# A decoder step on one core: mixed tiles kept in SBUF, sums of squares inside the output product, half of a norm's remainders on GpSimd

## The reference

```
att   = rmsnorm(diff_attention(...), g_head) * (1 - lam_init)
glu   = gelu(s5_scan(...)) @ w_glu
mixed = sigmoid(gate_a) * (att @ w_attn_up) + sigmoid(gate_s) * (glu[:2048] * sigmoid(glu[2048:]))
x     = x + mixed @ w_out
h     = rmsnorm(x, g_ffn)
x     = x + peer_ffn(h)      # queries h @ w_query, product keys, 128 x 128 single-neuron experts
x     = x + (p @ w_ple) * sigmoid(rmsnorm(x, g_ple) @ w_ple_gate)
```

## Time and profile before

| what | us |
| --- | --- |
| median of 3 runs | 4635.27 (4634.18 to 4642.76) |
| the profiled execution | 4642.33 |
| its span | 4640.6 |
| TensorE busy (matmuls) | 4358.9 (94%) |
| DVE busy | 2641.2 (57%) |
| GpSimd busy | 2535.1 (55%) |
| ACT busy | 1537.7 (33%) |

### The profile page before, as it was taken

How to read it: one execution, slowest core, us unless ns; L and a number is a source line. 1 busy time by engine, 2 the same in 40 slices (tenths; PEclk the granted TensorE clock), 3 DMA queues, 4 the chain that set the end, 5 groups by cost and what they waited for, 6 DMA issues and landing times. The chain is left out here.

```text
span 4640.6 us, 80519 instructions
## 1 busy us (share of the span) xinstructions
PE 4358.9 (94%) x29764; PEld 4156.5 (90%) x29764; DVE 2641.2 (57%) x4339; ACT 1537.7 (33%) x2344; POOL 2535.1 (55%) x1826
## 2 busy tenths in 40 slices
PE   7899976999998898999999999999899999999999
PEld 5788875888787897999999999999899999999899
DVE  4477764554434302679566666655576767767621
ACT  3122213443443323223333333333333333333232
POOL 5687751322222342445566666657566666666543
PEclk9999987999999998999999999999899999999999
DMA  4233322334984532333589999979888888878533
GB/s 113 71 94 93 94 62 89 104 100 125 375 316 148 192 111 75 99 92 129 199 314 340 328 344 323 346 256 332 306 323 328 336 331 320 340 281 335 210 97 95
DMA packets 365052, 993.54 MB, mean 214 GB/s; under 512 B 43922, under 2 KB 121490, under 8 KB 305970
## 3 DMA queue, kind: packets, MB, share of 16 engines
q1 hardware_dynamic: 268370, 554.21, 36.1%
q0 software_dynamic: 46560, 337.14, 18.7%
q10 hardware_dynamic: 49920, 99.47, 5.6%
HBM read 904.93 MB, written 85.72 MB: 213 GB/s over the span
## 5 line engine op out<-in xcount | busy, mean ns | idle before, releaser
L2774 PE MATMUL val_y_ps<-val_wt,val_v 128*128 128x384 f32 x6144 | 1074.2, 335 | 30.4 <-DVE val_wt L2848 23.7
L2774 PEld LDWEIGHTS val_y_ps<-val_wt,val_v 128*128 128x128 f32 x6144 | 1068.0, 188 | 36.1 <-issue 31.4
L248 PE MATMUL rt_acc<-xn_act,rt_w_hi 128*128 128x384 f32 x4096 | 1062.8, 340 | 31.0 <-POOL rt_w_rest L238 30.7
L238 POOL TENSOR_TENSOR rt_w_rest<-rt_w_raw,rt_w_hi 128x512 fp32r<-128x512 f32 x576 | 736.9, 1304 | 509.5 <-ACT rt_w_hi L233 507.2
L248 PEld LDWEIGHTS rt_acc<-xn_act,rt_w_hi 128*128 128x128 f32 x4096 | 739.1, 188 | 46.3 <-POOL rt_w_rest L238 42.6
L2736 POOL TENSOR_TENSOR val_v<-val_v_raw,val_v 128x2048 fp32r<-128x2048 f32 x128 | 591.0, 4617 | 327.1 <-ACT val_v L2807 327.0
L248 PE MATMUL rt_acc<-xn_act,rt_w_rest 128*128 128x384 f32 x2048 | 691.8, 338 | 0.0
L2651 DVE CUSTOM_DVE_ANT_0 rt_space<-rt_space,rt_mid 128x2048 f32<-128x2048 f32 x160 | 360.9, 2280 | 216.1 <-DMA rt_space<-in_peer_u,out_row_id 208.5
L2869 DVE TENSOR_TENSOR out_xT<-out_xT,val_y_ps 128x384 f32<-128x384 f32 x512 | 282.3, 551 | 339.6 <-PE val_y_ps L2774 339.4
L233 ACT ACTIVATE rt_w_hi<-rt_w_raw 128x512 fp32r<-128x512 f32 x576 | 334.6, 627 | 283.3 <-PE rt_acc L248 196.7
L248 PEld LDWEIGHTS rt_acc<-xn_act,rt_w_rest 128*128 128x128 f32 x2048 | 383.7, 187 | 0.0
(11 more groups left out here) (428 smaller groups left out, 7308.8 us busy)
## 6 DMA issues: line engine op xcount, KB each, us to landing
rt_w_raw<-in_peer_uT SPq DMA_DIRECT2D x512, 256.0 KB, 5.2
val_v_raw<-in_peer_vp SPq DMA_DIRECT2D x128, 1024.0 KB, 5.0
scan_w_raw<-in_w_in SPq DMA_DIRECT2D x128, 256.0 KB, 3.2
att_w_raw<-in_w_in SPq DMA_DIRECT2D x96, 256.0 KB, 3.4
hid_scratch<-rt_hid ACTq DMA_DIRECT2D x128, 192.0 KB, 6.2
gate_scratch<-rt_space ACTq DMA_DIRECT2D x12, 2048.0 KB, 10.3
val_hid<-hid_scratch SPq DMA_DIRECT2D x32, 768.0 KB, 8.3
val_gate<-gate_scratch SPq DMA_DIRECT2D x32, 768.0 KB, 11.5
```

The costliest lines, as they stand in the source:

```text
L238: e.tensor_tensor(self.rest[:, s, 0:nk, :], self.raw[:, r, 0:nk, :], self.hi[:, s, 0:nk, :].bitcast(F32), ALU.subtract).then_inc(self.rest ...
L248: mm = e.matmul(acc[:, h, 0:width], w[:, s, k, :], act[:, kt0 + k, a, col + h * width:col + (h + 1) * width], start=first and k == 0 and w ...
L2774: mm = e.matmul(y_ps[:, t % 2, 0:DW], v[:, c % 2, a, j, t * P:(t + 1) * P], wt[:, g % 2, j, b, :], start=j == 0 and a == 0 and b == 0, sto ...
```

## The change

Four edits:

1. `xT` is allocated at the outset; `early` and `qk_sample` become views of it, since its 34 KB are just theirs. `stage_mix` writes the mixed tile straight into `xT[:, c]`. The ring `mix`, the 16 stores, their waits and `mix_dram` go. `stage_out` makes high part and remainder from `xT`, and fetches the residual's input over a pair of tiles once their remainders are made, after the loads of the odd column of the pair.
2. In `stage_out` ACT interleaves the splits of the first four weight units with the copies (after tiles 0, 4, 8 and 12 instead of 3, 7, 11 and 15). All loops are unrolled.
3. The squares and the sums over them move from the norm into `stage_out`: ACT squares tile c-2 after the first weight split of column c, and TensorE sums tile c-1 after the third unit of column c; the last two squares and the last sum stand at the end. The sums' accumulator `end` is allocated outside both stages.
4. In `Norm`, the ring of scaled tiles grows from 2 to 4; DVE scales one tile ahead; the remainders of odd tiles are made by GpSimd, after its fourth weight remainder; the query product waits for even and odd ones.

```diff
@@ -291,82 +291,69 @@
...
-    def squares(self, e, landed=None):
...
     def split(self, e):
-        e.wait_ge(self.sq_used, KT)
-        e.activation(halves(self.sq[:, 0, :]), self.total[:, :, 0:HALF], ACT.Copy, scale=1.0 / 32
+        e.activation(halves(self.part[:]), self.total[:, :, 0:HALF], ACT.Copy, scale=1.0 / 32
                      ).then_inc(self.part_ready, 1)
...
+        for t in range(KT):
+            e.wait_ge(self.scaled_ready, t + 1)
+            e.activation(self.out[:, t, 0, :], self.scaled[:, t % 4, :], ACT.Copy).then_inc(self.hi_ready, 1)
...
-        for k in range(KT):
-            e.wait_ge(self.sq_ready, k + 1)
-            square_sum(e, self.total, self.sq, self.c("ones"), k).then_inc(self.sq_used, 1)
...
     def wait_tiles(self, e, n):
-        e.wait_ge(self.scaled_free, n + 2)
+        e.wait_ge(self.rest_even, n // 2)
+        e.wait_ge(self.rest_odd, n // 2)
+    def rest(self, e, t, done):
+        e.wait_ge(self.hi_ready, t + 1)
+        e.tensor_tensor(self.out[:, t, 1, :], self.scaled[:, t % 4, :], self.out[:, t, 0, :].bitcast(F32),
+                        ALU.subtract).then_inc(done, 1)
+    def odd_rests(self, e):
+        for t in range(1, KT, 2):
+            self.rest(e, t, self.rest_odd)
     def vector(self, e):
         e.wait_ge(self.dev_ready, 1)
         e.reciprocal(self.rstd[:], self.deviation[:]).then_inc(self.rstd_ready, 1)
         e.wait_ge(self.rstd_ready, 1)
         e.wait_ge(self.gain_in, 16)
...
+        def scale(t):
+            if t >= 4:
+                e.wait_ge(self.rest_odd if t % 2 else self.rest_even, t // 2 - 1)
+            e.scalar_tensor_tensor(out=self.scaled[:, t % 4, :], in0=self.x[:, t, :], scalar=self.gain[:, t:t + 1],
+                                   in1=self.rstd[:], op0=ALU.mult, op1=ALU.mult).then_inc(self.scaled_ready, 1)
+        scale(0)
+        for t in range(0, KT, 2):
+            scale(t + 1)
+            if t + 2 < KT:
+                scale(t + 2)
+            self.rest(e, t, self.rest_even)
...
-                if part == ATT and c:
-                    store(c - 1)
-            store(KT - 1)
-            for a in range(2):
-                e.wait_ge(mix_stored[a], 16 * (KT // 2))
@@ -2074,12 +2051,10 @@
...
-                if c >= 2:
-                    e.wait_ge(mix_stored[c % 2], 16 * (c // 2))
...
-                e.tensor_tensor(mix[:, c % 2, :], a_part[:], x, ALU.add).then_inc(mix_ready, 1)
+                e.tensor_tensor(k.xT[:, c, :], a_part[:], x, ALU.add).then_inc(mix_ready, 1)
...
@@ -2098,82 +2073,86 @@
...
         @block.sync
         def _(e):
+            for c in range(KT):
+                for u in range(U):
+                    w.load(e, 0, 0, c * U + u, columns(k.w_out, c, UNIT * u))
+                if c % 2:
+                    e.wait_ge(rest_ready, c + 1)
+                    e.dma_start(k.xT[:, c - 1:c + 1, :], k.x_dram[:, c - 1:c + 1, :]).then_inc(x_in[c // 2], 16)
+        @block.gpsimd
+        def _(e):
+            w.credit_rest(e)
+            for u in range(KT * U):
+                w.split_rest(e, 0, 0, u)
+        @block.scalar
+        def _(e):
+            def square(t):
+                e.wait_ge(added, t + 3)
+                if t >= 4:
+                    e.wait_ge(sq_used, t - 3)
+                e.activation(sq[:, t % 4, :], k.xT[:, t, :], ACT.Square).then_inc(sq_ready, 1)
             for t in range(KT):
...
+                e.activation(k.act[:, t, 0, :], k.xT[:, t, :], ACT.Copy).then_inc(hi_ready, 1)
+                if t % UNIT == 0:
+                    w.split_hi(e, 0, 0, t // UNIT)
+            for u in range(RING, KT * U):
+                w.split_hi(e, 0, 0, u)
+                if u >= 2 * U and u % U == 0:
+                    square(u // U - 2)
+            for t in range(KT - 2, KT):
+                square(t)
         @block.tensor
         def _(e):
             w.credit_used(e)
...
+            def sums(t):
+                e.wait_ge(sq_ready, t + 1)
+                square_sum(e, k.end, sq, k.c("ones"), t).then_inc(sq_used, 1)
+            for c in range(KT):
+                e.wait_ge(added, c + 1)
+                for u in range(U):
+                    if c == 0:
+                        e.wait_ge(rest_ready, (u + 1) * UNIT)
+                    w.multiply(e, 0, 0, c * U + u, acc[c % 2], k.act, u * UNIT, u == 0, u == U - 1)
+                    if c and u == 2:
+                        sums(c - 1)
+            sums(KT - 1)
         @block.vector
         def _(e):
...
+            e.sem_inc(added, 2)
             for t in range(KT):
                 e.wait_ge(hi_ready, t + 1)
...
+                e.tensor_tensor(k.act[:, t, 1, :], k.xT[:, t, :], k.act[:, t, 0, :].bitcast(F32),
                                 ALU.subtract).then_inc(rest_ready, 1)
...
+            for c in range(KT):
+                e.wait_ge(x_in[c // 2], 16)
+                w.wait_used(e, 0, 0, (c + 1) * U)
+                x = halves(k.xT[:, c, :])
+                e.tensor_tensor(x, x, acc[c % 2][:, :, 0:HALF], ALU.add).then_inc(added, 1)
...
+        scaled, part_sums, deviation, rstd = ranks.take(4, TOK), ranks.take(TOK), ranks.take(TOK), ranks.take(TOK)
...
+        end = k.end
+        norm = Norm(s, k.xT, k.g_ffn[0], k.act, k.c, end, (part_sums, deviation, rstd, scaled))
@@ -2317,6 +2296,8 @@
...
             for u in range(base(FIRST_B)):
+                if u == 4:
+                    norm.odd_rests(e)
                 w.split_rest(e, 0, 0, u)
...
@@ -2366,8 +2347,6 @@
...
                 for u in range(PER_A):
-                    if u == 0 and first:
-                        norm.squares(e)
                     w.split_hi(e, 0, 0, i * PER_A + u)
...
-    k.mix_dram = nc.dram_tensor("mix_scratch", [KT, P, TOK], F32).ap()
+        k.xT = s.sb("xT", [P, KT, TOK])
-            k.qk_sample = s2.sb("qk_sample", [P, 2, NH, NS])
+            k.qk_sample = k.xT[:].rearrange("p k n -> p (k n)")[:, NPG * NH * P:KT * TOK].rearrange(
+                "p (j h n) -> p j h n", j=2, h=NH)
-            early = s2.sb("early", [P, NPG * NH * P])
+            early = k.xT[:].rearrange("p k n -> p (k n)")[:, 0:NPG * NH * P]
...
-            k.xT = s4.sb("xT", [P, KT, TOK])
+                k.end = s5.ps("end", [P, 2, 512])
```

103 lines of the change are left out of this document (11 added, 92 removed).

## The result

The kernel became slower, by a little: the median of 11 executions of the changed kernel is 4650.43 us, of the kernel before beside it 4637.60 (11). The ratio is 1.0028 with a 95% interval of 1.0018 to 1.0039, so +8 to +18 us. The prediction was 4641.0 us with a range of 4630 to 4650, and "no change" (less than 0.2%) the likeliest outcome. It was wrong: the median lies 9.4 us above the forecast and just outside the range, and the kernel became slower by 0.28%.

A forecast was written before the change was run, and what follows sets the result against it. TensorE, busy 94% of the span, was taken to bound the kernel; -11.8 + 16.5 + 2.2 - 3.8 + 0.8 + 1.8 = +5.7 us on the median 4635.27 gave 4641.0 us, range 4630 to 4650.

The forecast's parts named there:

- the entry: Start of the output product, last mixed tile to first addition: shorter without the DRAM round trip, -11.8 us (-12.9 to -9.9).
- the lone sums: Inside the output product: 15 single-tile pairs of float32 matmuls in TensorE's busy queue, 1.1 us each, +16.5 us.
- Rival 2: Sums inside the output product nearly free at 0.28 us a tile, 4.2 instead of 16.5; 4628.7 us, chance 0.06.
- rival 3: Sums inside the output product: width changes drain the array, 1.5 us or more a tile; 4647.0 us, chance 0.13.
- Exit: End of the output product: last tile's square, hops and pair of matmuls after the last addition, +2.2 us (1.8 to 2.9).
- start: Start of the norm: squares gone, partial sums read 8.6 us after SP's first load instead of 12.45, -3.8 us.
- the norm's tiles: Tiles of the norm: DVE and GpSimd take turns at SBUF, 3.25 us a pair instead of 3.1, +1.8 us together.
- The sum over partitions: Start of the norm: this sum finds TensorE at half clock, 2.0 us instead of 1.19, +0.8 us.
- rival 1: Norm's tiles: ports not exclusive, odd remainders run beside DVE; sum -2.4 us, 4632.9 us, chance 0.11.
- Rival 4: Entry not shortened by the change: weights land 6 us after issue, TensorE starts at 1598.5; +3 us, 4644, chance 0.08.

The follow-up runs named there:

- e3: The changed kernel with the sums of squares in groups of four tiles instead of one tile per column; ratio to the kernel before 0.9997 (0.9989 to 1.0006).
- e8: The changed kernel with the two halves of a tile's sum on two different quarters of the array; ratio to the kernel before 1.0021 (1.0013 to 1.0030).
- e12: The changed kernel run again without any edit, for a second profile and set of times; ratio to the kernel before 1.0039 (1.0026 to 1.0052).
- e7: The changed kernel with ACT's partial-sum read and square root ahead of the route stage's four weight splits; ratio to the kernel before 1.0017 (1.0008 to 1.0025).
- e4: The changed kernel with the norm's odd remainders back on DVE, all else kept; ratio to the kernel before 1.0017 (1.0008 to 1.0025).

## Why the prediction was wrong

**Two terms failed, both towards slower: the entry was taken 2.6 us too good and the lone sums 2.0 us too cheap.** The other four together are 0.8 us the other way, which makes the 3.8 us between +5.7 and +9.5. The signs and places were right. The sums were the largest term; taken at 1.1 us, they cost 1.24 each (+18.5 instead of +16.5), at the upper bound that I had given (1.25). Of the 1.1, the changes of width were a guess of 0.1 at each side; e3 and e8 give 0.3 for both. The Trainium skill's rule that I cited for it, TensorE: Matmul & The Clock Gate, Part 3, that matmuls overlap when each has its own part of the array, is borne out in its place: 4, 4 and 16 instructions in 1.10, 0.65 and 1.14 us on one, two and four quarters. Rival 2 (nearly free) fell; rival 3 had the right side and too high a price (1.5 us a tile).

**The entry was the step that failed first:** -9.2 instead of -11.8. Two parts of it did. "with 2.9 I get 1591.6" took the landing from the old stage's first transfer, a mixed tile; the first weight unit needs 3.7 (why was not tried), which is the 0.8 us by which TensorE starts late. And "the last about 1605.5, and unit 3 wants it at 1607" let the tiles run ahead of TensorE. I had allowed 10.0 us from the fourth remainder to the last, some 1.2 us of it for GpSimd; it took 13.0, since DVE's remainders take 1.05 us each over fifteen beside GpSimd's weight remainders. TensorE's third and fourth units waited 2.3 us for them, and 0.8 came back because the granted clock was at 1.0 again 3.6 us after the first matmul, and not at the end of unit 0 (5.45).

**Exit, start and the norm's tiles** came out near the forecast (+1.8, -4.05, +0.5, +1.9 against +2.2, -3.8, +0.8, +1.8), but the last two by luck. The sum over partitions at half clock cost 1.0 us more (2.18 instead of 1.19), and 0.46 came back between reciprocal and first product, where DVE had been idle for 0.50 ahead of its loop; I had put the unrolling at nothing. And the pair of tiles costs 3.11 us, not 3.25, so first product to last unit took 25.46 us, not 26.6: +0.7 instead of +1.8. The other +1.2 is the last unit at half clock, which e12's profile of the same kernel doesn't have. The Trainium skill, in SBUF — State Buffer, "SBUF: two separate sides", says that a DVE operation with two SBUF inputs and a GpSimd operation that reads SBUF exclude each other; the changed kernel and e7 show the lock in numbers (1.48 to 2.55 us for two products, 2.18 to 5.28 for three), so rival 1 fell. What I missed is that the same edit also took DVE's wait for ACT away: with all remainders on DVE a pair costs 2.67 us against 3.08 (e4). Rival 4 fell too: TensorE started 9.1 us after the last mixed tile, not 11.3.

**The range was too narrow above.** Local terms give +9.5 where I had +5.7; the median moved by 12.8, with an interval of 8 to 18. Whether the other 3 us are a cost outside the edited stretch, or a profile of the kernel before whose stretch was 3 to 4 us longer than in three others with the same entry and norm, stays open. I had allowed nothing for stages that aren't edited, though all code behind moved, and nothing for the granted clock falling at one small wait or another.

## What to carry to other kernels

Put small matmuls of another shape between full ones only in groups that fill the array: here the visit cost nearly the same for one tile as for four, so fifteen visits cost 18.5 us and three cost 3.9. Before giving DVE's work to GpSimd, look whether the operations read two SBUF inputs; here they did, the help cost 0.44 us a pair of tiles, and DVE alone with a deeper ring was the fastest. Take more than one profile of the kernel before: kernels with the same entry and norm differed by 3 to 4 us in this stretch, as much as most terms of this sum. And where an engine's queue holds weight work ahead of the one short operation that starts a long chain, move that operation to the front.

## What the runs showed of the hardware

- A float32 matmul of 32 columns by 272 rows is two instructions; four in a row on one quarter of the array follow each other at 0.23 us and cost a busy TensorE 1.24 us (changed kernel), two by two on two quarters 0.78 (e8), sixteen on four quarters 1.29 (e3).
- A DVE product that needs 0.74 us alone took 1.76 on average beside GpSimd's weight remainders (e7: three in 5.28), and GpSimd's own remainder of 544 columns took 1.75 beside two DVE products, which took 2.55 (changed kernel).
- In TensorE's pause at the entry the granted clock fell to 0.5, and it came back 3.6 us after the first matmul; in the kernel before, it had come back 5.7 us after the first matmul and fell once more at 1616.9, in a wait of 2.76 us, for 3.4 us.
- One kernel's clock differs between executions: the changed kernel's last unit of the query product took 4.36 us in one profile and 3.09 in another (e12).
